# Chunk hybrid step: a later GpSimd preparation, added TensorE turns and a shifted low part

## The reference

```python
def layer(x, c, attn_fn, wkv0, shift0, ...):
    sh1, sc1, gt1, sh2, sc2, gt2 = split(silu(c) @ w_ada + b_ada, 6)
    h = rmsnorm(x, g_norm[0]) * (1 + sc1) + sh1
    z = h @ w_in                       # q, k, v | RWKV columns zs | 2 x 1024 gates
    gates = sigmoid(z[..., gate columns])
    o_a = attn_fn(q, k, v, rel_bias)   # own 64-frame chunk and the 8 before it
    zx = zs + (prev - zs) * mu         # token shift
    o_b, wkv1 = rwkv7_time_mix(zx, wkv0, ...)
    merged = gates[..., :D] * (o_a @ w_out_attn) + gates[..., D:] * (o_b @ w_out_rwkv)
    x = x + gt1 * (merged @ w_out)
    h2 = rmsnorm(x, g_norm[1]) * (1 + sc2) + sh2
    u, gg = split(h2 @ w_ffn_in, 2)
    x = x + gt2 * ((silu(gg) * u) @ w_ffn_out)
    return x, k, v, wkv1, zs[:, -1]

def rwkv7_time_mix(...):               # per head, S is 64 x 64
    S_t = S * w_t - (S kk_t) (kk_t a_t)^T + v_t k_t^T ;  y_t = S_t r_t
    y = group_norm(y) + sum(r k r_k) v ;  return y * g, S
```

## Time and profile before

| | |
|---|---|
| time, median of 3 runs | 1065.28 us (1063.9 to 1068.2) |
| the profiled execution's own time | 1063.88 us |
| its span in the trace | 1061.1 us |
| mean granted TensorE clock over the span | 0.983 |
| PE busy | 1011.6 us, 95% |
| PEld busy | 930.9 us, 88% |
| DVE busy | 529.2 us, 50% |
| ACT busy | 445.9 us, 42% |
| POOL busy | 362.1 us, 34% |

### The profile page before, as it was taken

One profiled execution on the slowest core, in us unless ns is written; L12 is line 12 of the kernel. 1 busy time (PEld: TensorE's weight loads), 2 busy tenths in 40 slices (PEclk: granted clock), 3 DMA queues, 4 the chain that ended last, 5 costly groups with the idle time before them and its releaser, 6 DMA issues.

```text
span 1061.1 us, 26246 instructions
## 1 busy us (share of the span) xinstructions
PE 1011.6 (95%) x10736; PEld 930.9 (88%) x10736; DVE 529.2 (50%) x1173; ACT 445.9 (42%) x983; POOL 362.1 (34%) x315
## 2 busy tenths in 40 slices
PE   5999999999998989899899999999999999999997
PEld 3899989899997767777787999999999999999997
DVE  5500000087025676666546646788888888900003
ACT  4443323353444444444523235555555555811112
POOL 2164433342233250600224156333332423043331
PEclk9999999999999999899999899999999999999999
DMA  9986756234411000002134342143324242233312
GB/s 356 375 280 229 251 189 222 81 123 144 145 43 48 13 13 12 13 12 85 44 119 139 94 184 80 48 112 96 102 80 117 79 118 67 83 85 97 92 55 85
DMA packets 118179, 122.28 MB, mean 115 GB/s; under 512 B 5396, under 2 KB 102848, under 8 KB 115656
## 3 DMA queue, kind: packets, MB, share of 16 engines
q1 hardware_dynamic: 112864, 111.86, 32.7%
q10 hardware_dynamic: 5224, 9.10, 2.6%
HBM read 108.33 MB, written 15.23 MB: 116 GB/s over the span
## 4 chain that ended last, share of the span: by engine, by line
PE 86%; DVE 7%; ACT 3%; issue 3%; POOL 1%; ACTq 1%; DVEq 0%; POOLq 0%
PE ps L1851 61%; PE ps L2448 21%; PE ps L2202 2%; DVE s_sb L1478 1%; PE ps L2102 1%; DVE s_sb L1512 1%; ACT x_sq L841 0%; DVE xn L1290 0%; POOL w_lo L658 0%; DVE Pb L1449 0%; DVE y_sb L1834 0%; POOL w_lo L809 0%; DVE XX L1459 0%; ACTq L827 0%; PE ps L1992 0%
## 5 line engine op out<-in xcount | busy, mean ns | idle before, releaser
L658 POOL TENSOR_TENSOR w_lo<-w_raw,w_hi 128x2048 fp32r<-128x2048 f32 x24 | 110.7, 4611 | 233.3 <-ACT w_hi L851 214.2
L1851 PE MATMUL ps<-hh,w_hi 128*128 128x274 f32 x832 | 176.6, 295 | 2.8 <-DVE hl L1300 2.0
L1851 PE MATMUL ps<-hl,w_hi 128*128 128x274 f32 x832 | 173.5, 291 | 1.0 <-DVE al L1793 1.0
L1851 PE MATMUL ps<-hh,w_lo 128*128 128x274 f32 x832 | 173.8, 291 | 0.0
L1851 PEld LDWEIGHTS ps<-hh,w_hi 128*128 128x128 f32 x832 | 132.3, 190 | 12.9 <-issue 11.2
L1851 PEld LDWEIGHTS ps<-hl,w_hi 128*128 128x128 f32 x832 | 132.3, 190 | 1.2 <-DVE al L1793 1.2
L1851 PEld LDWEIGHTS ps<-hh,w_lo 128*128 128x128 f32 x832 | 132.3, 190 | 0.8 <-issue 0.8
L803 POOL TENSOR_TENSOR ws_lo<-w_raw,ws_hi 128x512 fp32r<-128x512 f32 x63 | 80.6, 1294 | 144.9 <-DVE ps L1711 130.3
L2448 PE MATMUL ps<-th,ws_hi 128*128 128x274 f32 x336 | 97.5, 290 | 0.0
L2448 PE MATMUL ps<-tl,ws_hi 128*128 128x274 f32 x336 | 97.4, 290 | 0.0
L2448 PE MATMUL ps<-th,ws_lo 128*128 128x274 f32 x336 | 97.1, 289 | 0.0
(11 more groups left out here) (425 smaller groups left out, 2282.4 us busy)
## 6 DMA issues: line engine op xcount, KB each, us to landing
w_raw<-in_w_ffn_in SPq DMA_DIRECT2D x44, 512.0 KB, 4.6
w_raw<-in_w_in SPq DMA_DIRECT2D x42, 512.0 KB, 5.1
ada_l<-in_w_ada SPq DMA_DIRECT2D x16, 1024.0 KB, 6.5
ada_w<-in_w_ada SPq DMA_DIRECT2D x8, 1024.0 KB, 13.5
w_raw<-in_w_ffn_out SPq DMA_DIRECT2D x16, 384.0 KB, 4.1
w_raw<-in_w_ffn_out SPq DMA_DIRECT2D x16, 320.0 KB, 3.4
g_d<-gst SPq DMA_DIRECT2D x16, 274.0 KB, 2.5
gring<-g_d SPq DMA_DIRECT2D x16, 274.0 KB, 3.0
```

What stands on the lines that cost most here:

```text
L658: pool.tensor_tensor(w_lo[:, s, 0:cols], w_raw[:, s, 0:cols], w_hi[:, s, 0:cols].bitcast(F32), ALU.subtract).then_inc(lo_done, 1)
L1851: return pe.matmul(out, lhsT, rhs, start=start, stop=stop)
```

## The change

1. **GpSimd, preparation.** For hp of 1 to 3 the prelude also waits until `x0_done` has reached (hp - 1) x TT + 2, that is, until VectorE has added the diagonal in both tiles of the first round of the pair before. `attn_low(hp - 2)` stands behind the 11 steps instead of ahead of them. The call behind the loop, `attn_low(HP - 2)`, stays.
2. **GpSimd, unit U_OB.** Its low part is made by four subtractions over 512 columns (`low_in_four`, moved up in the text, unchanged) instead of one over 2048.
3. **TensorE, turns.** `idle_turns(b, n)` is new: n transposes of the 128 x 128 identity into bank b, whose results nobody reads. There are five calls: A, 12 after `early(0)`; B, 12 after `early_flip(0)`; C, 12 in the first round (g == 3) before the level steps, behind a wait for `s_biased` of 1; D, 10 after `attn_tile(7)`, for which the wait on `yc_done` stands ahead of the one on `rs8`; E, 8 after the third `spread`.
4. **VectorE, merged tiles.** The low part `mgl(i)` is made one tile later: behind the gate and the sum of tile i + 1, the last one behind the loop.

```diff
@@ GpSimd
+            def low_in_four(i, s):
+
+                pool.wait_ge(hi_done, i + 1)
+                pool.wait_ge(unit_mm, i - 1)
+                for b in range(0, UC, UC // 4):
+                    ins = pool.tensor_tensor(w_lo[:, s, b:b + UC // 4], w_raw[:, s, b:b + UC // 4],
+                                             w_hi[:, s, b:b + UC // 4].bitcast(F32), ALU.subtract)
+                ins.then_inc(lo_done, 1)
...
             for hp in range(HP):
-                if hp >= 2:
-                    attn_low(hp - 2)
                 if hp:
                     pool.wait_ge(sc_mm, (hp - 1) * TT)
                     pool.wait_ge(gm_dve, (hp - 1) * TT)
+                    pool.wait_ge(x0_done, (hp - 1) * TT + 2)
                     for k in range(11):
                         prelude(pool, link, hp, k)
+                    if hp >= 2:
+                        attn_low(hp - 2)
...
-            low(U_OB, U_OB % 2)
+            low_in_four(U_OB, U_OB % 2)
@@ VectorE
+            def merged_low(i):
+
+                dve.wait_ge(mgh_done, i + 1)
+                tt(mgl[:, i, :], mt1[:, i, :], mgh[:, i, :].bitcast(F32), ALU.subtract).then_inc(mg_done, 1)
             for i in range(KD):
...
                 dve.sem_inc(g_used, 1)
-                dve.wait_ge(mgh_done, i + 1)
-                tt(mgl[:, i, :], mt1[:, i, :], mgh[:, i, :].bitcast(F32), ALU.subtract).then_inc(mg_done, 1)
+                if i:
+                    merged_low(i - 1)
+            merged_low(KD - 1)
@@ TensorE
+            def idle_turns(b, n):
+
+                for _ in range(n):
+                    pe.transpose(ps[:, b, 0:P], ident[:, :], ident[:, :])
...
             early(0)
+            idle_turns(4, 12)
             rstd_spread()
             for n in range(1, 4):
                 early(n)
             early_flip(0)
+            idle_turns(ACC[0], 12)
...
                 if 3 <= p < 13:
+                    if g == 3:
+                        pe.wait_ge(s_biased, 1)
+                        idle_turns(6, 12)
                     for n in (a, b):
...
             attn_tile(7)
+            pe.wait_ge(yc_done, HP)
+            idle_turns(0, 10)
             pe.wait_ge(rs8, 1)
-            pe.wait_ge(yc_done, HP)
...
             for m in range(3):
                 spread(m)
+            idle_turns(2, 8)
```

More of the change, by code:

```diff
@@ L781, in token_low @@
                 ins.then_inc(tl_done, 1)
-            def low_in_four(i, s):
-                pool.wait_ge(hi_done, i + 1)
-                pool.wait_ge(unit_mm, i - 1)
-                for b in range(0, UC, UC // 4):
-                    ins = pool.tensor_tensor(w_lo[:, s, b:b + UC // 4], w_raw[:, s, b:b + UC // 4],
-                                             w_hi[:, s, b:b + UC // 4].bitcast(F32), ALU.subtract)
-                ins.then_inc(lo_done, 1)
             for i in range(U_WO, U_UP + 1):
```

## The result

The changed kernel takes 1052.07 us (median of 6 runs, 1049.38 to 1053.18) against 1064.75 us for the kernel before (6 runs, 1063.9 to 1068.2). The medians differ by 12.7 us, or 1.2%; the ratio formed from all runs is 0.9872, with a 95% interval of 0.9855 to 0.9888. So it is faster, clear of the noise. I had forecast 1058.2 with a range down to 1054.0, so the sign was right and the gain nearly twice as large as my sum.

The account below looks back on a forecast made before the run. TensorE was taken as the bound (86% of the chain), losing time at half clock. Terms -1.5 - 0.6 - 3.5 + 0.4 + 0.85 - 2.7 = -7.05 gave 1056.8 profiled, 1058.2 us as median; range 1054.0 to 1064.0.

Parts of the forecast that it names:

- A: Twelve turns after `early(0)`, in TensorE's 2.18 us idle before 17.43 us: 1.44 us fit in, VectorE decides, 0.
- B: Twelve turns after `early_flip(0)`, in the gap before 27.61 us: half-clock stretch from 29.1 sped up, -1.5 us.
- C: Twelve turns in the first round, before 336.25 us: -0.6 us, a third of the gain; ends -1.7 and +0.7.
- D: Ten turns behind the last attention tile: no idle TensorE to fill, first spread delayed, +0.85 us; ends 0 and +1.2.
- E: Eight turns before RWKV tile 0, in the 1.31 us gap: stretch from 585.5 at full clock, -2.7 us.
- The preparation on GpSimd: Later prelude in second and third pair ends collisions with VectorE's diagonal steps: -3.5 us, half of 7.05; ends -7.05 and 0.
- the whole excess goes: Rival: the heads' whole excess vanishes, also the half clock behind it: -7.05 instead of -3.5, 1054.7 us; chance 0.13.
- Low part in four: Unit U_OB: four subtractions take 5.02 us against 4.62 for one, delaying VectorE's gating steps: +0.4 us.
- Merged low part: Low part `mgl` made one tile later, from 595 us on where TensorE paces the loop: 0.
- The rule on transposes: Skill's rule that transposes don't earn full clock: B, C and E would bring nothing, sum -2.25; opening's row spoke against it.
- "Slower": turns at half clock: Rival: turns at 0.24 us each overrun their gaps, 5.4 us plus 0.4 of the low part: 1071.1; chance 0.04.

## Why the prediction was wrong, step by step

- **B.** Forecast -1.5, start of the rounds 1.68 us earlier, the stretch from 29.1 at full clock: right in size. No run leaves out A or B alone, so the gain is theirs together. Among the profiled executions with both, the rounds started at 330.6 to 331.4, among those without at 332.3 to 335.1. The spread of 0.8 us has a cause that the prediction didn't have: in six of these ten the clock fell shortly ahead of B's turns, at 24.5 to 25.2 us, and stayed at half for 3.4 us. B's twelve turns then took 2.4 to 2.8 us instead of 1.47, and TensorE had no idle time left before the first product.
- **C.** Forecast -0.6 within -1.7 and +0.7; the first round is 1.30 us shorter. The gain is real, the cause isn't shown to be C: the kernels without C that were profiled had 23.84 to 23.99 us too, except the kernel before (25.16) and the one with GpSimd's order alone (25.15). The feared delay by the later prelude didn't come: the round takes 23.84 us with it and 23.98 without (turns alone).
- **The preparation on GpSimd.** This is the step that failed. I had read 7.05 us too much in the second and third pair and taken half, "-3.5", with no row for the half. Measured -8.38, beyond even the end of -7.05. Two parts of it were wrong. First, the half: I thought that the prelude's products would collide with the next VectorE steps as they did with the diagonal step. The steps L1444, L1450 and L1460 (L1443, L1449 and L1459 before) read PSUM and weren't longer (0.29 us at 385.92 under a running product). Only the scaling L1512/L1513 can meet it, and it met it before the change too (0.93 us then, 0.38 and 0.81 now). Second, the yardstick: I took the fourth pair's 8.69 us as clean, but it has a collision of its own; freed of theirs, the other two take 8.08, so 0.61 us of excess in each pair was missing from my 7.05. The rival "the whole excess goes" had the right mechanism, 0.13 of the chance, and 1054.7 us. The split by experiment: 3.2 us collisions, 5.2 us the clock that fell behind them. I had the clock's possible share in the text (4.8 us in the third pair) and didn't add it up: 1.6 us of collisions in each of the two pairs, plus the half clock of 1.4 us in the second and 3.75 in the third, is what the forecast should have carried.
- **Low part in four.** Forecast +0.4, measured +0.45 in the stretch, by the way described: VectorE's gating ends later by what `x_lo` ends later.
- **D.** Forecast +0.85. Measured 0.85 both with the pieces (16.88 - 16.03) and without them (16.44 - 15.59). Right, and `sqy` now waits for TensorE, 1.03 us.
- **E.** Forecast -2.7. The profile of the changed kernel gives -2.2 with 3.4 us of half clock left; without D -3.0, at full clock; without E the stretch takes 44.11 us. So the size was right where the clock stayed up, and that isn't always: of the nine profiled executions with E's turns five were at full clock here, two at half clock for 3.4 us and two for 6.8; those of the five kernels without E, the one before among them, were at half clock for 3.3 to 10.2 us. The turns make the full clock likelier, as these counts read, but they don't secure it.
- **Merged low part.** Forecast 0; at most 0.2 us. **A.** Forecast 0; the clock from 18.9 to 22.3 rose to full, but the first product started only 0.16 us earlier.
- **The rule on transposes.** The clearest row stands in the kernel with the whole low part and without D. The clock had fallen at 24.5 us, while TensorE was idle; then nothing but transposes ran until the first product at 28.15, and the clock was full from 27.9:

```profile
24.50:27.80 3.30, 2.78 (x13) 2.78 (x14) 1.28 (x5) 0.94 (x3) 0.00 (x0) 0.50 1.03 405
27.90:28.10 0.20, 0.20 (x4) 0.20 (x2) 0.20 (x2) 0.20 (x1) 0.00 (x0) 1.00 1.17 471
```

```profile
25.02 1.12 PE L1932 MATMUL ps<-ident,ada_sb 128*128 128x128 f32 x4 [1.04 <-DVE ada_sb L1326]
25.93 2.44 PE L1864 MATMUL ps<-ident 128*128 128x128 f32 x12
28.15 0.36 PE L1857 MATMUL ps<-hh,w_hi 128*128 128x274 f32 x1
```

At the end of the changed kernel, where TensorE is idle from 1041 us, the clock falls near 1043.6 and is still at 0.50 at 1049, so it doesn't come back by itself within such a time. By the Trainium skill, "TensorE: Matmul & The Clock Gate", Part 4, PE-mode transpose, a transpose isn't counted as TensorE's activity the way a matmul is, and the full clock isn't granted for it; its figures there are for bf16. The trace of these float32 transposes disagrees with it. The opening, which I had put against the rule, can't decide: the granted clock reads 1.00 all through it, whatever its transposes last.
- **"Slower": turns at half clock.** It happens: E's eight turns took 1.93 us in the changed kernel's profile and used up their gap, and B's twelve took up to 2.77 us in six others, whose first product began 0.4 to 0.8 us later than the changed kernel's (27.45). The price stayed under 1 us; the rival had all five groups at half clock and came to 5.4.

With the measured -8.4 in place of -3.5 my sum would have been -11.95 and the time 1053.3. Of the rest of the way to 1052.07, 0.7 us are the first round (-1.3 where I had -0.6), and 0.5 the kernel before itself, whose median over six runs is 1064.75 and not 1065.28.

**What stays open.** Which of the possible places falls to half clock in an execution. The start fell in six of the ten profiles with B. The fourth pair fell in two kernels (GpSimd alone, without C) and in no other; the stretch behind the third spread was at full clock in the kernels with turns only (with D), without D (three of them) and without C, and at half clock for 3.4 us in both profiles of the changed kernel, and for 6.8 us in the one with C's and D's turns left out and in the one with all turns and the fourth pair's subtraction moved. Neither C nor D decides it alone, and no experiment here controls it. The best version measured is the changed kernel without D (1048.94 us), with the whole low part and the fourth pair's subtraction moved (1048.70): 3 us under the changed kernel, and the two can't be told apart.

## What to carry to other kernels

When a half-clock stretch follows a wait, price the wait and the stretch separately: in this kernel 1.6 us of waiting in a round was followed by half clock that cost up to 3.75 us, and removing the wait on the helper engine was worth more in these two rounds (8.4 us) than filling the gap with turns (5.2 us). Check a yardstick for the very fault that you want to price: the stretch that I took as clean had a collision of 0.6 us in it. Look for a VectorE step that takes several times its usual duration and ends just behind a GpSimd operation; move the GpSimd operation, and see what it meets in its new place, or cut it into pieces. Filler turns pay only in a gap that is really idle, and not in every execution; ten of them ahead of work that was ready cost their full length less the slack, 0.85 us.

## What the runs showed of the hardware

- A VectorE step whose operands are all in SBUF (the diagonal step, the scaling, the gating) lasted until shortly behind the end of the GpSimd operation then running: 1.58 us instead of 0.43 beside a 1.36 us operation, 0.67 us when that operation was cut into pieces. Steps that read PSUM kept their duration, 0.29 us at 385.92 under a running GpSimd product.
- Transposes of the identity, as TensorE's only work, brought the granted clock back from 0.50 to 1.00 (at 27.9 us, without D and with the whole low part), and with twelve of them in the second and third pair it stayed at 1.00 over the rounds that otherwise had 3.4 to 10.2 us at 0.50 or 0.51. They don't always do: the clock fell 0.3 us behind E's turns in one kernel (574.4 us).
- The clock's falls are not the same in every execution of one kernel: the changed kernel's first six executions lay near 1049.6 us (two) and at 1052.1 to 1053.2 (four), at mean clocks of 0.996 to 0.997 and 0.993 to 0.994.
